# Moving one fetched block of a weighted row sum from TensorE to VectorE in the last pass of a hybrid block

## What is computed

```python
PEER_HEADS = 8; PEER_TOPK = 16; PEER_EXPERTS = 128 * 128; D_MODEL = 1024; SEQ = 1024

def peer_ffn(h, w_q, sub_keys, expert_down, expert_up):
    ...
        idx = i1 * PEER_KEYS + i2                    # 8 heads x 16 picks = 128 experts per token
        g = jax.nn.softmax(cv, axis=-1)
        u = expert_down[idx]
        act = jax.nn.gelu(jnp.einsum('thkd,td->thk', u, xb).astype(jnp.float32), approximate=False)
        v = expert_up[idx]
        return jnp.einsum('thk,thkd->td', (g * act).astype(xb.dtype), v)
...
x = x + gate2 * rms_norm(y_ffn, norm_post_ffn[l])
```

## Time and profile before

| | |
|---|---|
| median of three runs | 4054.26 us (4047.75 to 4057.29) |
| profiled execution | 4050.82 us |
| its span, first to last instruction | 4049.1 us |
| TensorE busy in the span | 3792.8 us, 94% |
| VectorE, ScalarE, GpSimd busy | 67%, 41%, 45% |
| `experts_up` in the trace | from 2981 us to the end |
| moved by DMA in the span | 956.88 MB, mean 236 GB/s |

### The profile page before, as it was taken

The page is one execution under the profiler, slowest core; times in us unless marked ns, Lnnn a source line. Parts: engine busy times, 40 slices in busy tenths (PEclk is TensorE's granted clock), DMA queues, the critical chain, the costliest instruction groups (busy, mean ns, idle before and its releaser), DMA issues. The chain is left out here.

```text
span 4049.1 us, 57327 instructions
## 1 busy us (share of the span) xinstructions
PE 3792.8 (94%) x21102; PEld 3191.3 (79%) x21102; DVE 2722.3 (67%) x4934; ACT 1659.1 (41%) x3219; POOL 1831.1 (45%) x1291
## 2 busy tenths in 40 slices
PE   6999899989899969989999999999969999999998
PEld 3877687866677868989999999999956777777776
DVE  3688411148775328988989889998756666666666
ACT  2111234358422431126777777777612222222222
POOL 3333233359544212133333333345546767676764
PEclk8999899999999989999999999999989999999999
DMA  4244323358666342267889899999989999999998
GB/s 159 69 154 148 121 97 125 101 164 258 190 185 194 104 130 63 68 220 251 281 270 286 283 288 285 296 291 301 349 303 351 350 348 353 337 341 350 350 348 292
DMA packets 640656, 956.88 MB, mean 236 GB/s; under 512 B 198788, under 2 KB 417812, under 8 KB 639508
## 3 DMA queue, kind: packets, MB, share of 16 engines
q1 hardware_dynamic: 310976, 406.43, 30.8%
q0 software_dynamic: 110592, 402.70, 28.4%
q10 hardware_dynamic: 218836, 144.47, 11.3%
HBM read 806.54 MB, written 146.93 MB: 235 GB/s over the span
## 5 line engine op out<-in xcount | busy, mean ns | idle before, releaser
L2054 POOL DMA_INDIRECT down_rows<-in_peer_down_dram,row_ids x384 | 475.5, 1238 | 794.4 <-DVE row_u L2194 700.7
L2075 PE MATMUL p_u<-h2T_hi,downT_hi 128*128 128x320 f32 x2048 | 654.4, 320 | 7.9 <-ACT gelu_out L2125 6.8
L2075 PE MATMUL p_u<-h2T_lo,downT_hi 128*128 128x320 f32 x2048 | 634.5, 310 | 0.0
L2075 PE MATMUL p_u<-h2T_hi,downT_lo 128*128 128x320 f32 x2048 | 633.9, 310 | 0.0
L2194 DVE CUSTOM_DVE_ANT_0 gate_rows<-down_rows,x_tok_rows 128x1024 f32<-128x1024 f32 x384 | 468.6, 1220 | 85.7 <-DMA down_rows<-in_peer_down_dram,row_ids 69.8
L2597 PE MATMUL p_y<-up_hi,coef_hi 128*128 128x512 f32 x1240 | 493.2, 398 | 16.3 <-DVE coef_lo L2489 9.2
L2597 PE MATMUL p_y<-up_lo,coef_hi 128*128 128x512 f32 x1240 | 485.7, 392 | 0.0
L2597 PE MATMUL p_y<-up_hi,coef_lo 128*128 128x512 f32 x1240 | 483.9, 390 | 0.0
L545 PE MATMUL p<-hT_hi,w_hi 128*128 128x512 f32 x1024 | 409.6, 400 | 7.1 <-POOL w_lo L499 7.1
L545 PE MATMUL p<-hT_hi,w_lo 128*128 128x512 f32 x1024 | 399.7, 390 | 0.0
L545 PE MATMUL p<-hT_lo,w_hi 128*128 128x512 f32 x1024 | 399.4, 390 | 0.0
(11 more groups left out here) (342 smaller groups left out, 8100.8 us busy)
## 6 DMA issues: line engine op xcount, KB each, us to landing
down_raw<-in_peer_down_dram SPq DMA_DIRECT2D x128, 512.0 KB
up_raw<-in_peer_up_dram SPq DMA_DIRECT2D x128, 512.0 KB
scratch_gu<-gelu_out ACTq DMA_DIRECT2D x128, 320.0 KB
gelu_in<-scratch_gu SPq DMA_DIRECT2D x128, 320.0 KB
weights_in<-scratch_w SPq DMA_DIRECT2D x128, 320.0 KB
w_raw<-in_w_in_dram SPq DMA_DIRECT2D x64, 512.0 KB, 4.2
scratch_w<-weights_out ACTq DMA_DIRECT2D x40, 512.0 KB
scratch_w<-y_acc ACTq DMA_DIRECT2D x40, 512.0 KB
```

Of the source, the lines that this page charges most:

```text
L2054: pool.indirect_dma_start(out=rows[:, c % RING, :], out_offset=None, in_=inp["peer_down"][0], in_offset=bass.IndirectOffsetOnAxis(ap=row_i ...
L2075: mm = pe.matmul(ps_u[half][:, 0:HD], d[:, n % 3, k, :], h2[h][:, k, half * HD:(half + 1) * HD], start=(j == 0), stop=(j == 3 * KD - 1))
```

## The change

`NP` goes from 2 to 1, so that only block 0 is summed on TensorE, and blocks 1 and 2 (`NO = 2`) are summed on VectorE. TensorE's quads become 32, one to a group, at slot 1; `add_own` becomes 256, eight in a group. The ring of `rows` shrinks from 6 to 4 buffers, that of `own_rows` grows from 2 to 4. In a group GpSimd still fetches 12 times: eight `fetch_own`, two after each cut, and four `fetch` in step 0 (in group 1 in step 3). VectorE's additions to the output are no longer spread 2, 3, 2, 3 over the four steps but 1, 2, 2, 5 (`ADDED_WITH`). The spread of a group is made one group earlier. `keep_rows` in the middle of the pass goes, as `range(NP - 1)` is empty. Each `add_own` after the first now waits for the one ahead of it directly, since two stand side by side.

```diff
-    NP = NA - 1
-    OWN = NA - 1
-    FINISH = (*range(NP - 1), OWN, *range(NA, TB - 2), NP - 1, TB - 2, TB - 1)
-    RING = 6
+    NP = NA - 2
+    NO = NA - NP
+    ADDED_WITH = (range(0, 1), range(1, 3), range(3, 5), range(5, SLOTS))
+    FINISH = (*range(NP - 1), *range(NP, NA), *range(NA, TB - 2), NP - 1, TB - 2, TB - 1)
+    RING = 4
     SPREADS = 2 * NP
-    RING_OWN = 2
+    RING_OWN = 4
...
                 for g in range(1, GROUPS):
-                    r, c = (g - 1) * 4 * NP + RING, (g - 1) * GT + RING_OWN
-                    cut(g, 0)
-                    fetch_own(c)
-                    for i in range(4):
-                        fetch(r + i)
-                    cut(g, 1)
-                    fetch_own(c + 1)
-                    cut(g, 2)
-                    fetch_own(c + 2)
-                    for i in range(4, 8):
-                        fetch(r + i)
-                    cut(g, 3)
-                    fetch_own(c + 3)
...
+                    c = (g - 1) * GT * NO + RING_OWN
+                    for j in range(GT):
+                        cut(g, j)
+                        for i in range(NO):
+                            fetch_own(c + j * NO + i)
+                        if j == (GT - 1 if g == 1 else 0):
+                            for i in range(4):
+                                fetch(4 * g + i)
...
                         coefs(g, j)
                         if g:
-                            add_own((g - 1) * GT + j)
+                            for i in range(NO):
+                                add_own(((g - 1) * GT + j) * NO + i)
                         if g == 0:
                             continue
-                        for s in range(j * SLOTS // GT, (j + 1) * SLOTS // GT):
+                        for s in ADDED_WITH[j]:
                             add(g - 1, s)
-                    for q in range(NP):
-                        spread_rows(g * NP + q)
+                    if g + 1 < GROUPS:
+                        for q in range(NP):
+                            spread_rows((g + 1) * NP + q)
...
-                for j in range(GT):
-                    add_own((GROUPS - 1) * GT + j)
+                for i in range(GT * NO):
+                    add_own((GROUPS - 1) * GT * NO + i)
...
-                            elif j % 2:
-                                quad(j // 2)
+                            elif j == 1:
+                                quad(0)
```

More of the change, by code:

```diff
@@ L2360, in fetch_own @@
                 def fetch_own(c):
+                    a, k = NP + c // P, c % P
                     if c == 0:
@@ L2377, in _ @@
                 cut(0, 1)
-                for r in range(4):
+                for r in range(RING):
                     fetch(r)
                 fetch_own(0)
+                fetch_own(1)
                 cut(0, 2)
                 cut(0, 3)
-                for r in range(4, RING):
-                    fetch(r)
-                fetch_own(1)
+                fetch_own(2)
+                fetch_own(3)
                 for g in range(1, GROUPS):
-                    r, c = (g - 1) * 4 * NP + RING, (g - 1) * GT + RING_OWN
-                    cut(g, 0)
-                    fetch_own(c)
-                    for i in range(4):
-                        fetch(r + i)
-                    cut(g, 1)
-                    fetch_own(c + 1)
-                    cut(g, 2)
-                    fetch_own(c + 2)
-                    for i in range(4, 8):
-                        fetch(r + i)
-                    cut(g, 3)
-                    fetch_own(c + 3)
-                for r in range((GROUPS - 1) * 4 * NP + RING, 4 * QUADS * NP):
-                    fetch(r)
-                for c in range((GROUPS - 1) * GT + RING_OWN, P):
+                    c = (g - 1) * GT * NO + RING_OWN
[6 more added lines that the diff above has]
+                                fetch(4 * g + i)
+                for c in range((GROUPS - 1) * GT * NO + RING_OWN, P * NO):
                     fetch_own(c)
@@ L2435, in _ @@
                         act.wait_ge(rows_kept, t + 1)
-                    elif t == OWN:
-                        act.wait_ge(own_added, P)
+                    elif t < NA:
+                        act.wait_ge(own_added, P * (t - NP + 1))
                     else:
@@ L2499, in add @@
                         dve.tensor_tensor(part, ps_y[s % BANKS][:], part, ALU.add).then_inc(added, 1)
+                for q in range(NP):
+                    spread_rows(q)
                 for g in range(GROUPS):
```

16 lines of the change are left out of this document (9 added, 7 removed).

## The result

| | before | changed |
|---|---|---|
| median | 4053.14 us (4047.75 to 4057.29, 4 runs) | 4146.51 us (4145.39 to 4149.49, 4 runs) |
| profiled execution | 4050.82 us | 4145.39 us |
| its span | 4049.1 us | 4143.7 us |

The median before is now of four runs, the three above and one beside the changed kernel. The changed kernel is slower, by a ratio of 1.0223 with a 95% interval of [1.0211, 1.0235]. The forecast was 4060 us in a range of 3980 to 4110, so the time lies 87 us over the one and outside the other. The direction that came, slower, was given 0.45.

The account below looks back on a forecast made before the run. TensorE was taken as full at 31.44 us a group; afterwards VectorE's 25.8 plus 4.7 holds plus 1.6 loads makes 32.1. 3044 + 963 + 50 = 4057 span, 4058.7 with surroundings, forecast 4060 us, range 3980 to 4110.

Parts of the forecast that it names:

- the start: Before the steady pass: group 1's steady work was to begin at 3044 us (3040 to 3049), against 3048.21 before.
- 30 groups: Middle of the pass: 30 groups at 32.1 us each were to take 963 us, against 953.7 before.
- the end: From the start of the last group to the finish: about 50 us, against 47.2 before.
- The step that failed: Last step of a group: loads issued near 21.5 us land in 5.5 to 7.5; the product waits up to 2.
- the holds of products, `coef_lo` and spread: VectorE standing behind GpSimd's cuts: about 4.7 us a group, on top of its 25.8 us of work.
- The wait for loads: VectorE's last product in a group waiting for its loads: 1.6 us a group.
- GpSimd's issue behind a sum: GpSimd's fetch issues in a group: 1.26 to 1.33 us each, 1.033 busy and 0.30 between.
- The slower case: Rival: last `coef_lo` of each group waits for loads released by the second cut; 33.4 us a group, 4101 us; chance 0.24.
- What TensorE waits for: TensorE, once per group: a wait of 2 to 3.5 us for `coef_lo`, in place of the quad.
- The clock: Part of the slower rival: TensorE, idle over 3 us a group, may come back at the lower clock.
- The transfers: Part-gain rival: transfers might bind at 30.5 or 30.9 us a group; 4017 or 4020 us; chance of part gain 0.22.
- VectorE's share: Sign of a right forecast: VectorE's busy share in the pass rises above 0.9, with hardly a wait for slots.

Follow-up runs that it names:

- x1: Changed kernel with gelu_in and weights_in loads issued ahead of the up_raw load in SyncE's queue: 4092.14 us, ratio 1.0098.
- x13: x9 with each cut replaced by two dependent one-input copies, low part left out: 4004.17 us, ratio 0.9867.
- x2: Changed kernel with the four quad fetches behind the second cut instead of the first, from group 2 on: 4113.92 us, ratio 1.0143.
- x6: Changed kernel with a fifth buffer for the rows VectorE sums and one fetch_own of each step ahead of the cut: 4073.34 us, ratio 1.0035.
- x3: Changed kernel with the additions spread 2, 3, 2, 3 over the steps as before: 4183.42 us, ratio 1.0324.
- x4: Changed kernel with each cut replaced by two dependent one-input copies, low part left out: 4064.48 us, ratio 1.0023.
- the cured kernel: Changed kernel with the edits of x6 and x1 together, computing everything: 4044.62 us, ratio 0.9969.
- x9: The cured kernel with the four quad fetches behind the second cut of a group instead of the first: 4111.54 us, ratio 1.0135.

## Why the prediction was wrong

By its own sum: the start was 3044 and came at 3053.9 (9.9 late); 30 groups were 963 and took 1042.7 (79.7 more); the end was 50 and took 4143.7 - 4096.7 = 47.0, 3.0 less. Together that is the 86.7 us between its span of 4057 and the 4143.7 measured, nearly all of it the group's length.

**The step that failed: "The loads of the last step are issued only when the second cut is done, near 21.5 ... so 5.5 to 7.5 us: they land between 27 and 29, and the last product waits up to 2 us for them".** In the turn shown, time 0 (the last `coef_lo` done) is 3536.30 - 34.81 = 3501.49. The second cut ended at 22.2, not 20.8, and the loads were in use at 31.0, 7.8 us after their issue. Of the 2.7 us between 32.1 and 34.8, 1.4 is the late cut and about 1.6 the longer time from the cut to the product; the rest came out 0.3 below. So both terms of this step were too small, by about as much. The other terms stood: the holds of products, `coef_lo` and spread are (1.161 + 1.220 - 1.64) x 4 + 1.726 - 0.33 = 4.4 us where 4.7 was said. The wait for loads is 4.3 us where 1.6 was said.

- *Why the cut was late.* GpSimd's issue behind a sum was counted at 1.26 to 1.33; it takes 1.94 plus 0.30 when it starts beside a second sum. It comes twice in a turn. The means and lone issues of the earlier trace rows hide it, but the trace of the kernel before has it, VectorE's row first:

```profile
3587.00 1.28 DVE L2479 SCALAR_TENSOR_TENSOR y_acc<-up_own_rows,row_coef,y_acc 128x1024 f32<-128x1024 f32 x1
...
3587.10 2.00 POOL L2356 DMA_INDIRECT up_rows<-in_peer_up_dram,row_ids_turned  x1 [0.30 <-issue]
```

- *Why the landing was long.* 8.4 us was in the earlier trace rows, and the forecast discounted it as the worst case, because hardly anyone waited mid-pass. That no one waits says that the load is issued early, not that it is short. With 8.4 us from 21.5 and the cut 1.4 later the forecast's own layout comes to some 35 us a group, an estimate from these rows; 34.76 was measured. In x1 and x13, where no loads of this kind are waited for, the median from issue to landing is 6.8 and 6.4 us, so the forecast's 5.5 to 7.5 fits the common load there, and not the one behind this cut, which took 7.8.
- *The rival.* The slower case described the mechanism that came: "It waits for loads that are released by the second cut, which now stands behind two sums and six DMA issues". It was priced at 33.4 us a group and 4101 us, 1.4 a group and 45 in all too low, and given 0.24. x1, x2 and x6, which cut the loop in three places, bear the mechanism out. Its rate, one microsecond a group for each of landing, no run varied by itself.
- *What TensorE waits for.* Not `coef_lo` but the addition of slot 5, which the lag puts behind the last coefficients and two sums. In x3, without the lag, it waits for `coef_lo`, and the kernel is 37 us slower.
- *The clock.* TensorE did come back slower (0.47 to 0.76 us for the first matmul of a group in the rows above, clock 0.94 over the stretch). The forecast let that add to the slow case; as TensorE is not in the loop, it adds nothing.
- *The start.* TensorE waits 5.07, 6.14 and 4.81 us in group 0 for additions that stand behind two sums each; before it waited 4.32 and 2.05. That is 9.7 us more where 2.5 was allowed for this and for late rows. Another 3.1 us lie ahead of group 0 (first matmul at 2993.91 against 2990.83). No run tested either.
- *The holds.* They were rightly weighed: x4, with copies for cuts, has products at 994 ns and `coef_lo` at 877, against 1161 and 1220. GPSIMD Engine Reference of the Trainium skill, section Key points, has VectorE instructions with two SBUF inputs contend with GpSimd, and the traces agree.
- *The transfers.* x13 moved 377 GB/s over 63 us. The 358 GB/s of the Trainium skill (DMA: Bandwidth & Descriptors, section Where 436 GB/s comes from) is no ceiling here.
- *VectorE's share* was to rise above 0.9; it is 730.2 / 943 = 0.77, because it waits. The list of signs did name the true sign: "waits for `weights_in` on VectorE of several us in every group".

What the quad is worth was right: 29.32 us is reached once the loop is open and the holds are short. Whether the remaining 2.0 us per group of the cured kernel can be had with true cuts is open; it would take cuts that do not meet two-input instructions, and none was found in the places tried.

## What to carry to other kernels

When work moves from an engine that is full to engines that have room, add up not their busy time but the turns: write down each wait whose release depends on the engine's own later work (buffer, load, sum, fetch), and go once round, with every latency at its largest measured value. Both values that were too small here, the load's 8.4 us and the issue's 2.0, stood in the trace of the kernel before. Cut such a loop where it is cheapest. Here reordering three loads in one queue and adding one ring buffer, with one fetch moved ahead of each cut, gave back 102 us. And a helper engine that runs ahead until its ring stops it is not free: its waits then fix which instructions of the other engine it holds.

## What was not expected of the hardware

- An indirect fetch whose issue on GpSimd starts while VectorE runs a sum of two SBUF inputs ends 0.8 us after that sum: 0.78 to 0.84 in the 139 such issues of the changed kernel's stretch. One that starts early in the sum takes up to 1.95 us instead of 0.94, one that starts near its end hardly longer. Means: 1258 ns with full sums in the changed kernel, 1002 with narrow ones, 958 in the kernel before.
- GpSimd's copies of one input hold VectorE's two-input instructions as well, only for their own, shorter length. The product took 2.03 us instead of 0.82 beside the copy below it (x13, VectorE and then GpSimd); beside a cut one took 3.41 (x9):

```profile
3514.64 2.03 DVE L2485 TENSOR_TENSOR gelu_in<-gelu_in,weights_in 128x640 f32<-128x640 f32 x1
...
3514.93 1.05 POOL L2376 CAST up_lo<-up_raw 128x1024 fp32r<-128x1024 f32 x1
```

- The awaited load took 7.8 us from issue to use in a pass that moves 317 GB/s in the mean. The mean hides that the transfers come in bunches: 350 GB/s at a DMA share of 0.96 in the 8.84 us up to its use, 264 at 0.77 later in the turn. How much of the landing is this bunching was not separated.
